# The last pair of each feed-forward group, turned by VectorE and transfers in place of TensorE, and a down stage in parts

## What is computed

```python
def _swiglu(h, w_gate, w_up, w_down):
    return (jax.nn.silu(h @ w_gate) * (h @ w_up)) @ w_down

x = x + _swiglu(_rms_norm(x, ffn_norm), w_gate, w_up, w_down)            # first block
...
mod = silu(c) @ ada_w + ada_b                                             # second block
sh1, sc1, g1, sh2, sc2, g2 = jnp.split(mod, 6, axis=-1)
...
h = rms_norm(x, ffn_pre_g) * (1.0 + sc2) + sh2
x = x + g2 * rms_norm(swiglu_ffn(h, w_gate, w_up, w_down), ffn_post_g)
```

## Time and profile before

| what | value |
|---|---|
| median of 3 runs | 2126.31 us (2125.09 to 2126.70) |
| the profiled execution | 2123.66 us |
| its span in the profile | 2121.8 us |
| PE busy | 2094.2 us, 99% of the span |
| DVE busy | 1593.2 us, 75% |
| ACT busy | 1088.7 us, 51% |
| mean granted clock of PE | 0.998 |
| HBM read | 510.15 MB, 241 GB/s over the span |

### The profile page before, as it was taken

One profiled execution on the slowest core, in us unless ns is written; L12 is line 12 of the kernel. 1 busy time (PEld: TensorE's weight loads), 2 busy tenths in 40 slices (PEclk: granted clock), 3 DMA queues, 4 the chain that ended last, 5 costly groups with the idle time before them and its releaser, 6 DMA issues.

```text
span 2121.8 us, 29253 instructions
## 1 busy us (share of the span) xinstructions
PE 2094.2 (99%) x9963; PEld 1828.6 (86%) x9963; DVE 1593.2 (75%) x2092; ACT 1088.7 (51%) x1529; POOL 216.8 (10%) x201
## 2 busy tenths in 40 slices
...
GB/s 282 232 206 197 205 80 316 284 323 316 309 305 305 313 324 297 307 303 320 285 153 211 191 224 159 255 250 252 320 316 266 204 212 214 211 201 203 210 213 152
DMA packets 376233, 526.46 MB, mean 248 GB/s; under 512 B 120856, under 2 KB 129432, under 8 KB 375856
## 3 DMA queue, kind: packets, MB, share of 16 engines
...
HBM read 510.15 MB, written 2.10 MB: 241 GB/s over the span
## 4 chain that ended last, share of the span: by engine, by line
PE 92%; DVE 3%; ACT 2%; DMA 1%; issue 1%; POOL 0%; SPq 0%; DVEq 0%; ACTq 0%; POOLq 0%
PE bank L1185 30%; PE bank L1201 29%; PE bank L1202 29%; DVE w_both L2284 1%; DMA raw<-in_w_in 1%; PE bank L1256 1%; PE bank L1289 0%; ACT w_both L1683 0%; PE bank L1277 0%; DMA x_t<-in_x_t 0%; ACT zsb L1624 0%; POOL convT L983 0%; ACT prob_mid L1735 0%; PE bank L1170 0%; PE bank L1326 0%
## 5 line engine op out<-in xcount | busy, mean ns | idle before, releaser
L2284 DVE TENSOR_TENSOR w_both<-raw,w_both 128x1024 fp32r<-128x1024 f32 x762 | 947.6, 1250 | 433.6 <-ACT w_both L1683 430.2
L1683 ACT ACTIVATE w_both<-raw 128x1024 fp32r<-128x1024 f32 x762 | 801.9, 1056 | 910.8 <-PE bank L1185 761.4
L1201 PE MATMUL bank<-w_both,act_hi 128*128 128x512 f32 x1984 | 754.2, 380 | 0.0
L1202 PE MATMUL bank<-w_both,act_lo 128*128 128x512 f32 x1984 | 751.9, 379 | 0.0
L1185 PE MATMUL bank<-w_both,act_hi 128*128 128x512 f32 x2160 | 552.5, 380 | 3.4 <-DVE w_both L2284 2.4
L1185 PEld LDWEIGHTS bank<-w_both,act_hi 128*128 128x128 f32 x2160 | 406.8, 189 | 62.9 <-DVE w_both L2284 3.7
L1201 PEld LDWEIGHTS bank<-w_both,act_hi 128*128 128x128 f32 x1984 | 375.0, 189 | 53.0 <-DVE act_lo L1964 0.2
L1202 PEld LDWEIGHTS bank<-w_both,act_lo 128*128 128x128 f32 x1984 | 375.0, 189 | 52.4
L1201 PE MATMUL bank<-w_both,mid_hi 128*128 128x512 f32 x960 | 366.3, 382 | 2.7 <-DVE mid_lo L2419 1.9
L1202 PE MATMUL bank<-w_both,mid_lo 128*128 128x512 f32 x960 | 364.4, 380 | 0.0
L2242 DVE SCALAR_TENSOR_TENSOR ada_acc<-ada_raw,c_act,ada_acc 128x512 f32<-128x512 f32 x360 | 269.8, 749 | 11.2 <-DMA ada_raw<-in_ada_w 4.2
...
## 6 DMA issues: line engine op xcount, KB each, us to landing
ada_raw<-in_ada_w SPq DMA_DIRECT2D x192, 512.0 KB, 5.6
raw<-in_w_gate SPq DMA_DIRECT2D x176, 512.0 KB, 4.6
raw<-in_w_up SPq DMA_DIRECT2D x176, 512.0 KB, 5.2
raw<-in_w_down SPq DMA_DIRECT2D x176, 512.0 KB, 4.7
raw<-in_w_in SPq DMA_DIRECT2D x166, 512.0 KB, 4.5
raw<-in_w_out SPq DMA_DIRECT2D x60, 512.0 KB, 5.3
h_tok<-h_blk SPq DMA_DIRECT2D x256, 32.0 KB, 4.5
...
```

The source lines that it names most:

```text
L1201: pe.matmul(pairs(A_[t]), h_, in_turn(w_hi[:, s, kk, :]), start=(k == 0), stop=False)
L1202: pe.matmul(pairs(A_[t]), l_, in_turn(w_hi[:, s, kk, :]), start=False, stop=False)
L1683: act.activation(w_hi[:, U % SPLIT_SLOTS].rearrange("p k n -> p (k n)"), raw_of(c, u).rearrange("p k n -> p (k n)"), ACT.Copy).then_inc(hi ...
L2284: dve.tensor_tensor(w_lo[:, U % SPLIT_SLOTS].rearrange("p k n -> p (k n)"), raw_of(c, u).rearrange("p k n -> p (k n)"), w_hi[:, U % SPLIT_ ...
```

## The change

The last pair of each group is turned like the others, by DVE's squares and sixteen transfers; `consume`, the copy L1651 and L2172 go. To give the transfers time, m0 and m1 run in two parts, in the order m0a, m1a, m0b, m1b, m2, m3: the b parts are the last two units of each, those whose rows are the last pair's. In a group of four pairs the six chunks have 6, 6, 2, 2, 8, 8 units, in a group of three 4, 4, 2, 2, 6, 6. SP issues four transfers behind each weight load of units 7 to 10 counted from m0a's first, and ACT and DVE make `mid_hi` and `mid_lo` after the last unit of m1a. PE waits for it at m0b. Where m0 and m1 carry loads of `ada_w`, m0a and m1a now do, in units 1, 2, 4 and 5 of six or 0, 1, 2 and 3 of four (`ADA_PART`). The sum of m0 is added after DVE's split of unit 1 of m2 (`ahead`), since m2 follows m0's end by two units only.

```diff
+    ADA_PART = {6: (1, 2, 4, 5), 4: (0, 1, 2, 3), 2: ()}
...
                 if prev and prev[0] == "up":
-                    TURNED_BEFORE[prev[1]] = by_turn[0]
-                    if f in BLOCKS_IN:
-                        blocks = dict(n=by_blocks[0], prev=prev, f=f)
-                        by_blocks[0] += trips
-                    else:
-                        by_turn[0] += trips
+                    blocks = dict(n=by_blocks[0], prev=prev, f=f)
+                    by_blocks[0] += trips
...
-                for h in range(2):
-                    m = 2 * p + h
-                    steps.append(chunk("w_down" + tag, m * CW, "mid", prev, k0=4 * done, nu=kc // KPU, ada=a[h],
-                                       pairs=pair0 + done + n, first="ffn" if m == 0 else None))
...
+            for half, units in enumerate((nu - 2, 2)):
+                kept = []
+                for m in range(2):
+                    if half == 1 and m == 0:
+                        pos["C"] -= 2
+                        kept = [pending.pop() for _ in pending[:]]
+                    ka = KPU * (nu - 2) * half
+                    c = chunk("w_down" + tag, m * CW, "mid", prev if half == 0 and m == 0 else None, k0=4 * done + ka,
+                              nu=units, ada=a[m] if half == 0 else None, ka=ka, half=half,
+                              first="ffn" if m == 0 else None, blocks=blocks if half == 0 and m == 0 else None,
+                              moved=blocks if half == 0 and m == 1 else None, **more)
+                    c["moves"] = {u: at_move + u - 7 for u in range(units) if 0 <= at_move + u - 7 < 4}
+                    c["closing"] = blocks
+                    at_move += units
+                    steps.append(c)
+                pending.extend(kept)
...
+            for m in (2, 3):
+                steps.append(chunk("w_down" + tag, m * CW, "mid", adds[m - 1], k0=4 * done, nu=nu, ada=a[m - 2],
+                                   ka=0, first=None, ahead=adds[0] if m == 2 else None, **more))
...
-    MOD_AT = next(c for c in S_FFN1 if "loop" not in c and c["ada"] and c["ada"]["row"] >= N_MOD)
+    MOD_AT = next(c for c in S_FFN1 if "loop" not in c and c["nu"] == NU and c["ada"] and c["ada"]["row"] >= N_MOD)
...
+                    if "closing" in c:
+                        if u in c["moves"]:
+                            for m in range(2 * c["moves"][u], 2 * c["moves"][u] + 2):
+                                move_blocks(c["closing"], r, m)
+                        continue
...
-                    for t in range(TT):
-                        for c in range(HPC):
-                            ins = pe.transpose(TURN[t][:, c * P:(c + 1) * P], zsb[:, t, c * P:(c + 1) * P], ident[:, :])
-                        ins.then_inc(h_turned, 1)
...
-                        pe.wait_ge(mid_lo_done, 2 * (c["pairs"] - (0 if u >= nu - 2 else 1)))
+                        pe.wait_ge(mid_lo_done, 2 * (c["pairs"] - 1 + c["half"]))
...
+                    if u == 1 and c.get("ahead"):
+                        pre(c["ahead"], c["C"] - 1, r)
```

100 lines of the change are left out of this document (41 added, 59 removed).

## The result

| what | before | after |
|---|---|---|
| median (lowest to highest) | 2126.27 us (2125.09 to 2126.70) | 2151.94 us (2150.26 to 2152.67) |
| profiled execution, its span | 2123.66, 2121.8 us | 2152.67, 2150.9 us |
| mean granted clock of PE | 0.998 | 0.992 |

Over four runs of each, the ratio is 1.0122, 95% interval 1.011 to 1.0134: 25.7 us slower. The forecast was 2139.5 us, 13.4 longer, with 2128 to 2147 as range. The sign was right, the size about half.

The account below looks back on a forecast made before the run. PE, busy 99% of the span, was taken to bound the kernel. Waits of 10.5 + 1.7 + 6.0 + 0.6 + 0.7 = 19.5 us less 6.1 gained made 13.4 us longer: 2139.5 us, range 2128 to 2147.

Parts of the forecast that it names:

- The gain, 6.1 us: Six down-stage groups: taking 48 closing turns from PE gains 5 × 0.88 + 1.74 = 6.1 us.
- the rival "hidden": Down stages: transfers stay hidden, no group is late, only the gain stays, 2120.2 us; chance 0.07.
- Sixteen transfers in 12.3 us, landing in 2.5: SP queue, units 7 to 10: sixteen transfers take 12.3 us to issue, 0.64 us each, and land 2.5 us after issue.
- Group 1.3, 10.5 us at unit 8: First unit of m0b in 1.3: PE waits 10.5 us, as transfers stand behind a modulation load awaiting a VectorE step.
- m0b of 1.1 and 1.2, 2.1 us: Unit 12 of groups 1.1 and 1.2: PE waits 2.1 us because unit 11's weight load is issued behind the transfers.
- 2.2, nothing, and 2.3, 0.7: First unit of m0b: no wait in group 2.2, which has no modulation loads; 0.7 us in 2.3.
- Group 2.1, 0.6 us: Group 2.1: the chain of 1.1 without the fold of sums and without loads in m2, 0.6 us wait.
- Behind m0b, 3.5 us: From m0b to m3: 0.9 us more wait at m2 in 1.1 and 1.2 each, and 1.7 us slow clock in 1.3.
- The clock, 1.7 us once: Group 1.3 after its wait: PE runs partly at 1.2 GHz, adding 1.7 us, charged once.
- The rival that issuing costs next to nothing: SP queue: only the weight loads' own 0.6 us paces the transfers, so the time would be 2122 us; chance 0.04.
- The sum: Whole kernel: waits of 19.5 us less 6.1 gained, 13.4 us longer, put on the median of 2126.31 us.
- My upper bounds: High ends of the forecast waits: about 4.3 us a group in 1.1 and 1.2, 1.9 us in 2.1.

Follow-up runs that it names:

- e11: Changed kernel with ScalarE sharing the transfers, 1.3's and 2.1's modulation loads in m2 and m3, m0's add before the step, mid_hi/mid_lo behind early m0b splits; 2120.0 us.
- e2: Changed kernel with the modulation loads and steps of groups 1.3 and 2.1 moved from m0a and m1a to m2 and m3; 2137.4 us.
- e3: Changed kernel with eight transfers in place of sixteen for each group's last pair, the other eight left out; 2141.3 us.
- e5: Changed kernel's down-stage order, but each group's last pair turned by TensorE's eight transposes as before, without transfers for it; 2136.8 us.
- e4: Changed kernel with m0's early add before the modulation step in m2, and GpSimd's sum in group 2.1 held until mid_lo is written; 2148.7 us.
- e7: Changed kernel with the last pair's sixteen transfers issued by ScalarE in place of SP in groups of four pairs; 2139.5 us.
- e6: Changed kernel with ScalarE issuing transfers in four-pair groups, 1.3's and 2.1's modulation loads in m2 and m3, and m0's add before m2's modulation step; 2127.6 us.
- e8: e6 with mid_hi and mid_lo of the last pair written after the splits of m0b's second unit in place of m1a's last; 2124.3 us.
- e1: Changed kernel with products into an unread bank put in front of PE's waits, to keep PE busy in them; 2150.5 us.

## Why the prediction was too low, step by step

- **The gain, 6.1 us: right.** In e11, where PE hardly waits, the six stages are 0.86, 0.74, 1.85, 0.88, 0.88 and 0.87 us shorter than before, 6.08 together, and the time is 2120.0; the rival "hidden" had 2120.2. The two profiled spans differ by 2.5 us only, since e11's is 3.6 us longer outside the stages; the 5.8 us are those of the medians.
- **Sixteen transfers in 12.3 us, landing in 2.5: right.** 12.6 us in 1.3; ACT's copy started some 2 us after the last was issued.
- **Group 1.3, 10.5 us at unit 8: right** (10.25 idle, 10.8 late), and for the reason given: e2 took it away by taking the modulation loads away. Issuing time and loads both count in it (e3, e5).
- **m0b of 1.1 and 1.2, 2.1 us: right** (2.4 and 2.1), by the late weight load of unit 11. **2.2, nothing, and 2.3, 0.7: right** (0 and 0.6).
- **Group 2.1, 0.6 us: wrong by 3.1.** I copied the chain of 1.1 and did not look at what GpSimd does beside VectorE at the new place; its sum made `mid_lo` 2.0 us longer (e4), and the other 1.1 us stays open. It was to be seen in the trace of before, where the same sum from 1625.55 on made one split last 1.82 us.
- **Behind m0b, 3.5 us: the step that failed, measured 13.3.** For 1.1 and 1.2 I followed the modulation load into m2 (step done 605.2, add 606.6) and let the weights of m2's first two units be there. They were not: the load of unit 17 is issued just in front of that modulation load, and its split on ACT and then DVE, 2.2 us, stands in front of the step. In 1.1 the add ended at 609.49, where the forecast had 607.0 (this group began 0.4 us later than in the trace of before): 2.5 us, and m2 began 5.5 us late, not 3.0. The reason lies further ahead: I had named the next split as what is queued behind ACT's and DVE's wait at m0b; queued were all the later weights. SP's 10 us of issuing use up the units split ahead, and the lead does not come back before m2, since slots come free only with the splits behind `mid_lo`.
- **How far that is shown.** With the sixteen on another queue (e7) 12.6 of the 17.9 us of 1.1, 1.2 and 2.1 go, but 8.0 of these at m0b, of which the forecast had 4.8. Of the 9.7 us behind m0b 4.6 go. The rest went with the order on DVE and ACT: with the add in front of the step 1.1 is on time at m2 (e6), with splits of m0b in front of the copies nearly all is gone (e8, 5.2 to 0.5). With no transfer for the last pair at all (e5), 1.1 and 1.2 still lose 1.4 and 1.3 us there.
- **The clock, 1.7 us once: too small.** It fell in four groups, and 8.3 of the 13.3 us behind m0b are slow units. But they are no term to add: e1 held the clock up, and 10.2 us were lost there all the same; the time fell by 1.5.
- **The rival that issuing costs next to nothing: refuted.** e3 halved the transfers and got 10.7 us. That halves what has to land too; e7, which moves the issuing and lands the transfers no sooner, decides it. The Trainium skill (DMA: Bandwidth & Descriptors, "Issuing engines are not separate DMA queues") says that starting DMAs on several engines saves only the sequencer's time, usually small beside the DMA. The runs agree on what is saved, not on its size: here that time was worth 12.5 us.
- **The sum** put a difference onto the median of before, which stands; the range ended 4.9 us too low. My upper bounds, 4.3 us a group for 1.1 and 1.2 and 1.9 for 2.1, were those of the waits that I had named, with none for weights running dry; measured were 5.6, 6.8 and 5.4. 1.3 and 2.3 stayed under theirs.

Open: 2.8 us of the spans' difference outside the six stages, which vary from kernel to kernel and were not tried.
